# Three-tap branch on GpSimd, transposes without diagonals, and new orders of the start, of the attention mixer and of the expert loop

## The chip, the cores and the metric

The kernel runs on one core of one Trainium2 chip. The metric is the device time of one execution in microseconds. Before the change the median of 3 runs is 2215.55 us (2214.48 to 2218.8).

## The reference

One sequence of 256 tokens with 1024 features, all in float32, passes through two blocks of two layers each.

The first block has two hybrid layers. Each one normalises x, projects it (`w_in`), runs three kinds of heads on it (a gated linear recurrence behind a four-tap convolution, causal attention with 4 heads of 64, and latent attention with 4 heads of 96), joins them with `w_out`, and adds an MLP of 4096 hidden features with a squared ReLU.

The second block is what most of the change touches:

```python
mod = silu(c) @ ada_w[i] + ada_b[i]                  # shifts, scales, gates sh1 sc1 g1 sh2 sc2 g2
h = rmsnorm(x, norm_g[i, 0]) * (1 + sc1) + sh1
y = conv_mixers(h) if i == 0 else attn_mixers(h)
x = x + g1 * y
h = rmsnorm(x, norm_g[i, 1]) * (1 + sc2) + sh2
x = x + g2 * hier_moe(h)

def conv_mixers(h):
    gate_b, gate_c, x_a, val_b, glu_gate = split(h @ w_in)          # 5 x 512 features
    y_a = gate_b * conv3(gate_c * x_a)                              # the three-tap branch
    u = conv31(val_b * sigmoid(glu_gate)) + bias                    # the 31 taps
    y_b = silu(layernorm(u, ln_g, ln_b))
    return concat([y_a, y_b]) @ w_out
```

`attn_mixers` has two kinds of heads over all 256 tokens: eight heads of 64 whose keys are limited to the 64 largest scores of a small index (8 heads of 32), and four differential heads (two softmax maps each, one subtracted with a factor lambda, then an RMS norm over 128). `hier_moe` picks for each token one group of 8 experts and two experts in it; each of 32 experts is a gated MLP of 512 hidden features. A last RMS norm ends it.

## The kernel before, in words

The program is written engine by engine, each with a fixed order of instructions, and the engines meet at semaphores only. A float32 product takes two TensorE instructions, a transpose one. Token tiles are t = 0, 1 of 128 tokens; `xres` holds x, `hT` its normalised transpose (8 tiles k of 128 features by 256 tokens), `bank` the eight PSUM banks, `B(i)` one of them. Intermediate results pass through banks 0 to 3 as numbered jobs (`JOBS`, `JOBS2`): TensorE fills one (`job_filled`), ScalarE drains it (`job_drained`), and a job may start when the one four before it is drained.

Weights pass through `ring`, slots of 2 MB. SyncE issues their loads in a fixed order, each behind a wait that its slot has been used.

Start (L381 to L436): SyncE loads x, then the condition vector, `ada_b`, small columns and positions, waits for GpSimd's constants (`consts`), loads 9 row pieces and 8 small pieces (`layer_small`), and then the first five ring units. TensorE (L757 to L786) turns the condition vector, waits for all the small pieces, turns the rows, turns x (`raw_transposes`) and starts with unit 0, `U_QK`. VectorE forms the rotary tables (L1671 on) before anything else.

Convolution mixer (TensorE L984 to L1001, VectorE L1998 to L2082): five projections `ab0` to `ab9`, two gate-row jobs, then `out_part(0)` for the three-tap half of `mixT`, products with ones for the layer norm (`ln_mu`, `ln_var`), and `out_part(1)` for the other half. VectorE starts the 31 taps when the inputs are drained, runs 24 of them over four channel groups of 256 tokens each (`conv_b(0, 24)`), then the three-tap branch (L2062 to L2067), and then the last 7 taps, centring, square, reciprocal and product, each over all 1024 columns.

`updated` (L1732, VectorE) adds a mixer's or the experts' output to x, one tile t of 1024 columns at a time, and squares it for the norm; GpSimd takes the root (`power2`, L620). `diagonal` puts the root on a diagonal matrix `dg2`, and `norm2` (L929, TensorE) multiplies x by it, which transposes and scales at once; `norm_drains` on ScalarE and `turned_drains` on VectorE scale it by columns into `hT`.

Experts (`moe`, TensorE L1003 to L1138): logits, a chain of small VectorE operations that picks experts and slots, then a loop `quad` over 8 groups of four experts, in two pairs each. Two experts of a pair share a product, one in each half of the array (`product`, L1056). A pair needs six ring slots: gate, up and down for both experts; SyncE refills a slot as soon as `g_filled`, `u_filled` or `y_filled` tells that it has been used (`moe_pairs`, L479). `gather` (L1041) brings tokens to the experts' slots by a product with a 0/1 matrix times the root (`pick`), `scatter` (L1050) adds the results back. VectorE also adds up the relative bias of the later attention in the first loop (`bias_of`).

Attention mixer (TensorE L1151 to L1241): gate row, index queries and keys, 8 index scores (`rel`), the projections `qc` to `vd`, and then four groups g of scores, softmax, transposes and values in turn; then lambda and norm, four transposes `cm`, and two output products. VectorE's softmax stands at L2298 to L2311, ScalarE's exponents at L1538 to L1547.

## Time and profile before

| what | us |
|---|---|
| median of 3 runs | 2215.55 |
| the profiled execution's own time | 2216.15 |
| its span, first to last instruction | 2214.4 |
| TensorE (PE) busy | 2063.9, 93% |
| VectorE (DVE) busy | 911.5, 41% |
| ScalarE (ACT) busy | 354.8, 16% |
| GpSimd (POOL) busy | 88.8, 4% |
| mean granted TensorE clock | 0.969 |

Busy TensorE is not TensorE at full speed: the instructions overlap, and at a granted clock of 0.5 (1.2 instead of 2.4 GHz) the same instruction is busy for twice as long. The profile reads from left to right as first block (to about 788), convolution mixer (to 922), first experts (946 to 1437), attention mixer (to 1686), second experts (1711 to 2202), last norm and store.

### The profile page before, as it was taken

How to read it: one execution, taken by the hardware profiler on the slowest of the kernel's cores; microseconds unless marked ns; L12 is line 12 of the kernel's file. 1: busy time of each engine (PE TensorE's matmuls, PEld its weight loads, DVE VectorE, ACT ScalarE, POOL GpSimd, SP SyncE). 2: the span in 40 equal slices, each digit the busy share in tenths (PEclk: the TensorE clock that was granted, in tenths of full speed). 3: DMA queues.
4: the chain of work that ended last, by engine and by line, in shares of the span. 5: the costliest groups of instructions: out<-in, count | busy, mean ns of one | idle time of the engine just before them, and what ended most of it. 6: DMA issues, size and time to landing. Idle time of an engine off the chain costs nothing. (4 is left out here: it accounts for less than half of the span.)

```text
span 2214.4 us, 21599 instructions
## 1 busy us (share of the span) xinstructions
PE 2063.9 (93%) x8170; PEld 1170.3 (53%) x8170; DVE 911.5 (41%) x1817; ACT 354.8 (16%) x744; POOL 88.8 (4%) x178
## 2 busy tenths in 40 slices
PE   6999999998999998699999999989878999999997
PEld 4556666555666676444444444367565444444442
DVE  3354551335455169466676667631334110111102
ACT  1421000132100000111111111111330111111110
POOL 1111110011111000000000000000000000000000
PEclk9999999999999999899999999979769999999999
DMA  6427884243688543269999999924211899999995
GB/s 227 152 79 266 313 321 165 93 149 112 249 304 304 182 150 152 79 260 410 411 408 408 408 424 415 363 82 145 83 76 76 341 411 409 408 408 410 408 408 237
DMA packets 109524, 592.65 MB, mean 268 GB/s; under 512 B 16664, under 2 KB 21271, under 8 KB 84887
## 3 DMA queue, kind: packets, MB, share of 16 engines
q1 hardware_dynamic: 96406, 541.48, 60.8%
q0 software_dynamic: 13056, 50.33, 6.0%
q8 instruction: 41, 0.67, 0.1%
q14 instruction: 21, 0.16, 0.0%
HBM read 590.74 MB, written 1.05 MB: 267 GB/s over the span
## 5 line engine op out<-in xcount | busy, mean ns | idle before, releaser
L1060 PE MATMUL bank<-ring,work 128*64 128x512 f32 x3072 | 676.4, 594 | 25.2 <-ACT work L1477 14.2
L1060 PEld LDWEIGHTS bank<-ring,work 128*64 128x64 f32 x3072 | 227.8, 137 | 439.1 <-issue 425.0
L2203 DVE SCALAR_TENSOR_TENSOR work<-work 128x512 f32<-128x512 f32 x384 | 258.6, 745 | 5.1 <-DVE work L2200 4.9
L731 PE MATMUL bank<-hT,ring 128*128 128x256 f32 x1024 | 223.4, 379 | 3.2 <-DVE hT L1603 3.2
L744 PE MATMUL bank<-ring,work 128*128 128x512 f32 x512 | 222.3, 592 | 0.0
L731 PEld LDWEIGHTS bank<-hT,ring 128*128 128x128 f32 x1024 | 194.4, 190 | 35.1 <-issue 9.4
L2207 DVE SCALAR_TENSOR_TENSOR work<-work,bank 128x512 f32<-128x512 f32 x32 | 22.0, 688 | 437.4 <-ACT work L1465 437.4
L1952 DVE SCALAR_TENSOR_TENSOR work<-ring,cond,work 128x512 f32<-128x512 f32 x168 | 126.3, 752 | 105.9 <-DMA ring<-in_ada_w 100.7
L744 PEld LDWEIGHTS bank<-ring,work 128*128 128x128 f32 x512 | 97.2, 190 | 115.5 <-issue 114.8
L1046 PEld LDWEIGHTS bank<-work,xres 128*128 128x128 f32 x512 | 124.6, 335 | 27.3 <-issue 22.7
L1046 PE MATMUL bank<-work,xres 128*128 128x256 f32 x512 | 133.5, 414 | 2.9 <-DVEq L2192 2.9
L666 PE MATMUL bank<-ring,hT 128*128 128x512 f32 (+1 forms) x320 | 135.0, 579 | 0.0
L951 PE MATMUL bank<-hT,ring 128*128 128x256 f32 x608 | 135.0, 385 | 0.0
L951 PEld LDWEIGHTS bank<-hT,ring 128*128 128x128 f32 x608 | 117.4, 194 | 17.6 <-issue 1.1
L1052 PE MATMUL bank<-work 128*128 128x512 f32 x256 | 119.6, 600 | 1.4 <-ACT work L1477 1.4
L666 PEld LDWEIGHTS bank<-ring,hT 128*128 128x128 f32 x320 | 59.8, 190 | 68.7 <-issue 68.5
L1458 ACT ACTIVATE work<-bank,modc,work 128x256 f32<-128x256 f32 x128 | 61.9, 564 | 119.9 <-PE bank L1046 119.9
L1052 PEld LDWEIGHTS bank<-work 128*128 128x128 f32 x256 | 46.3, 192 | 54.8 <-issue 51.2
L1382 ACT ACTIVATE work<-bank 128x512 f32<-128x512 f32 x32 | 19.1, 597 | 349.9 <-PE bank L731 349.9
L1477 ACT ACTIVATE work<-bank 128x512 f32<-128x512 f32 x64 | 38.2, 597 | 185.7 <-PE bank L1060 185.7
L2213 DVE SCALAR_TENSOR_TENSOR work<-work,bank 128x512 f32<-128x512 f32 x32 | 22.0, 687 | 110.1 <-PE bank L1060 110.1
L867 PE MATMUL bank<-ring,hT 128*128 128x512 f32 x128 | 59.1, 616 | 4.4 <-ACT hT L1264 2.6
(365 smaller groups left out, 1548.1 us busy)
## 6 DMA issues: line engine op xcount, KB each, us to landing
ring<-in_moe_w_gate SPq DMA_DIRECT2D x64, 2048.0 KB, 11.8
ring<-in_moe_w_up SPq DMA_DIRECT2D x64, 2048.0 KB, 15.3
ring<-in_moe_w_down SPq DMA_DIRECT2D x64, 2048.0 KB, 12.1
ring<-in_ada_w POOLq DMA_DIRECT2D x48, 1024.0 KB, 9.2
ring<-in_w_up SPq DMA_DIRECT2D x16, 2048.0 KB, 13.1
ring<-in_w_down SPq DMA_DIRECT2D x16, 2048.0 KB, 10.0
ring<-in_w_in SPq DMA_DIRECT2D x10, 2048.0 KB, 7.7
ring<-in_cd_w_in SPq DMA_DIRECT2D x6, 2048.0 KB, 8.6
```

The lines of the kernel that those rows point to most:

```text
L666: last = pe.matmul(b[:, 0:n], (hT if x is None else x)[:, k, t * P:t * P + P], w[:, k, 0:n], start=(k == kk - 1), stop=(k == 0))
L731: last = pe.matmul(B(4 + b)[:, (c % 2) * S:(c % 2) * S + S], w[:, k, c * P:c * P + P], hT[:, k, :], start=(k == 0), stop=(k == DT - 1))
L744: last = pe.matmul(B(2 * t + hf), uT[:, u % 2, k, t * P:t * P + P], w[:, k, 512 * hf:512 * hf + 512], start=(u == 0 and k == 0), stop=(u = ...
L867: last = pe.matmul(B(2 * t + hf), mT[:, 4 * u + k, t * P:t * P + P], w[:, k, 512 * hf:512 * hf + 512], start=(u == 0 and k == 0), stop=(u ...
L951: last = pe.matmul(b[:, (c % 2) * S:(c % 2) * S + S], w[:, k, c * P:c * P + P], hT[:, k, :], start=(k == 0), stop=(k == DT - 1))
L1046: last = pe.matmul(b[:, (d % 2) * S:(d % 2) * S + S], xres[:, t, d:d + DT * (P - 1) + 1:DT], pick[:, t, :], start=(t == 0), stop=(t == TT ...
L1052: last = pe.matmul(B(2 * t + hf), pgT[:, t * P:t * P + P], ye[:, 512 * hf:512 * hf + 512], start=False, stop=True, skip_group_check=True)
L1060: last = pe.matmul(b[h, :], x[:, k, h], w[e][:, k, c0:c0 + 512], start=(k == 0), stop=(k == kk - 1))
L1458: ins = act.activation(xeT[:, d, :], b[:, (d % 2) * S:(d % 2) * S + S], ACT.Identity, scale=gm[:, 2 * i + 1, d:d + 1], bias=sh[:, d:d + 1])
L1477: act.activation(ye[:, 512 * hf:512 * hf + 512], (G, U)[hf], ACT.Copy).then_inc(m["y_drained"], 1)
L1952: ins = dve.scalar_tensor_tensor(ada_acc[:, c % 2, :], ada_w[hf][:, k, :], cond[:, kk:kk + 1], ada_acc[:, c % 2, :], ALU.mult, ALU.add)
L2203: mo.do(dve.scalar_tensor_tensor(fl(bias[:, h]), mask_b, rbt[:, bass.ds(12 * bk + h, 1)], fl(bias[:, h]), ALU.mult, ALU.add))
```

## The change

- **Start.** SyncE loads x, the nine row pieces and then the ring units; the other small pieces go out between the ring units (`between`). TensorE turns x and starts unit 0 without waiting for the small pieces; the condition vector is turned between its halves. The tables are formed behind the first norm (`first_tables`), and GpSimd makes the constants that TensorE needs first.
- **First block.** The drains of `hT` are waited for one by one also for k of 4 and 6, and the sums of tile 1 go in halves of 512 columns, with `out_half` and `down_half` counting halves.
- **Norms of the second block.** `norm2` is made of plain transposes (`turn`) of x scaled into `xn` (`scaled_first` on ScalarE, `scaled_second` on VectorE). Ahead of the experts x is turned unscaled; the scale of columns goes into the router's weights (`router`), the root into the logits, and x, scaled and with its features in the order of the gather, is copied to `xn` by ScalarE (`scaled_for_gather`).
- **Convolution mixer.** GpSimd runs the three-tap branch. VectorE runs the 31 taps without a break, and the layer norm goes by channel groups; squares are ScalarE's.
- **Expert loop.** The scatter of a pair stands behind the next pair's hidden product, in both pairs; the gather comes in four pieces before the last down product; a first scatter adds zeros, a last one stands behind the loop.
- **Attention mixer.** Index scores stand between the first projections, the last four projections between the softmax groups, the output's first half before group 3 is done, the gate row behind it. Lambda is applied to the sums' inverses, and the last norm goes by tiles.

The core of the diff:

```diff
+            def short_branch():                                          # GpSimd
+                pool.wait_ge(s2["cols_done"], 1)
+                pool.wait_ge(s2["job_drained"], JOB2["ab7"] + 1)
+                own.do(pool.tensor_tensor(pa[:, :, 2:2 + S], abx[1][:, :, :], abx[2][:, :, :], ALU.mult))
+                own.wait()
+                for w in range(3):
+                    for c in range(4):
+                        tap = colsA[:, A_CA + 4 * w + c:A_CA + 4 * w + c + 1]
+                        own.do(pool.tensor_scalar(abx[2 if w else 1][:, c, :], pa[:, c, w:w + S], tap, None, ALU.mult))
+                    if w:
+                        own.wait()
+                        own.do(pool.tensor_tensor(abx[1][:, :, :], abx[1][:, :, :], abx[2][:, :, :], ALU.add))
+                    own.wait()
+                pool.wait_ge(s2["job_drained"], JOB2["ab9"] + 1)
+                pool.tensor_tensor(mixT[:, 0:4, :], abx[1][:, :, :], abx[0][:, :, :], ALU.mult).then_inc(s2["ya_ready"], 1)
...
-            conv_b(0, 24)                                                # VectorE
-
-            drained("ab7")
-            do(dve.tensor_tensor(pa[:, :, 2:2 + S], abx[1][:, :, :], abx[2][:, :, :], ALU.mult))
-            wait()
-            do(conv(abx[1], pa, 3, 0, 3, lambda w, c: colsA[:, A_CA + 4 * w + c:A_CA + 4 * w + c + 1], None))
-            wait()
-            drained("ab9")
-            dve.tensor_tensor(mixT[:, 0:4, :], abx[1][:, :, :], abx[0][:, :, :], ALU.mult).then_inc(s2["ya_ready"], 1)
-
-            ins = conv_b(24, 31)
-            wait()
-            ins.then_inc(s2["u_ready"], 1)
+            conv_b(0, 30)
+            for c in range(4):
+                dve.scalar_tensor_tensor(abx[3][:, c, :], pb[:, c, 30:30 + S], colsB[:, 120 + c:121 + c], abx[3][:, c, :],
+                                         ALU.mult, ALU.add).then_inc(s2["u_ready"], 1)
+            dve.wait_ge(s2["job_filled"], JOB2["ln_mu"] + 1)
+            total = B(OWN_BANK["ln_mu"])[:, 0:S]
+            for c in range(4):
+                dve.scalar_tensor_tensor(abx[3][:, c, :], total, -1.0 / 512, abx[3][:, c, :], ALU.mult, ALU.add).then_inc(s2["uc_ready"], 1)
...
-            out_part(0, AB_OUT, 6, landed2, mixT)                        # TensorE
+            out_part(0, AB_OUT, 6, landed2, mixT, ROW0 + ROW1[:1])
...
+            over_channels("ln_mu", "u_ready", abx[3])
+            out_part(0, AB_OUT, 6, landed2, mixT, ROW1[1:], 0, 2)
+            over_channels("ln_var", "uq_ready", abx[4])
+            out_part(0, AB_OUT, 6, landed2, mixT, ROW1[1:], 2, 4)
+            pe.wait_ge(s2["y_ready"], 1)
+            out_part(1, AB_OUT, 6, landed2, mixT, ROW0 + ROW1, 0, 1)
+            pe.wait_ge(s2["y_ready"], 4)
+            out_part(1, AB_OUT, 6, landed2, mixT, ROW0 + ROW1, 1, 4)
...
+            def turn(t, src):
+                for c in range(DT):
+                    last = pe.transpose(B(4 + c // 2)[:, (c % 2) * S + t * P:(c % 2) * S + t * P + P], src(c), ident[:, :])
+                    if t == 1 and c % 2:
+                        last.then_inc(s2["xT_filled"], 1)
...
+                    for j in range(2):                                   # quad
+                        pr = 2 * it + j
+                        hidden(it, j)
+                        pe.wait_ge(m["pg_drained"], pr + 1)
+                        scatter(0)
+                        hidden_turned(pr)
+                        scatter(1)
+                        if j == 0:
+                            pe.wait_ge(m["pickg_ready"], it + 1)
+                        gates_turned(it, j)
+                        down(pr, 0)
+                        if more and j == 1:
+                            pe.wait_ge(m["p_ready"], it + 2 + i)
+                            pe.wait_ge(m["pg_drained"], pr + 2)
+                            gather(0, X)
+                            gather(1, T)
+                            pe.wait_ge(m["xt_drained"], 4 * it + 5)
+                            gather(2, X)
+                            pe.wait_ge(m["xt_drained"], 4 * it + 6)
+                            gather(3, T)
+                        down(pr, 1)
...
+            for nm, unit, heads in (("qc0", 1, (0, 1)), ("qc1", 1, (2, 3)), ("kc0", 2, (4, 5)), ("kc1", 2, (6, 7)), ("vc0", 3, ()), ("vc1", 3, ()), ("qd0", 4, ())):
+                projection(nm, unit)
+                for h in heads:
+                    relevance(h)
+            scores2(0)
+            projection("qd1", 4)
+            p_transposes2(0)
+            projection("kd0", 5)
+            values2(0)
+            scores2(1)
+            projection("kd1", 5)
+            p_transposes2(1)
+            projection("vd0", 6)
+            values2(1)
+            scores2(2)
+            projection("vd1", 6)
+            p_transposes2(2)
+            mixed(0)
+            mixed(1)
+            values2(2)
+            scores2(3)
+            drained2("od01")
+            pe.wait_ge(s2["x_done"], 2)
+            out_part(0, CD_OUT, CD_RING, landed3, hT, ROW0)
+            p_transposes2(3)
+            out_part(0, CD_OUT, CD_RING, landed3, hT, ROW1)
+            values2(3)
+            gate_row(["gate1a", "gate1b"], 3)
+            mixed(2)
+            mixed(3)
+            for t in range(TT):
+                drained2("cm%d" % (2 + t))
+                out_part(1, CD_OUT, CD_RING, landed3, hT, (ROW0, ROW1)[t])
```

## Rows read from the trace of the kernel before

**Rows 1.** Page, busy time by engine: us (share of the span) xinstructions.

```profile
PE 2063.9 (93%) x8170; PEld 1170.3 (53%) x8170; DVE 911.5 (41%) x1817; ACT 354.8 (16%) x744; POOL 88.8 (4%) x178
```

**Rows 2.** Windows: stretch, us, each engine's busy us (instructions), PEclk, DMA share, GB/s.

```profile
865.00:921.60 56.60, 37.48 (x81) 17.44 (x80) 28.44 (x51) 7.15 (x10) 0.73 (x2) 0.82 0.44 181
921.60:946.00 24.40, 18.10 (x98) 15.48 (x98) 17.06 (x73) 3.43 (x8) 0.73 (x2) 0.93 0.29 93
946.00:1437.00 491.00, 473.56 (x2016) 211.32 (x2016) 323.68 (x578) 75.31 (x144) 0.00 (x0) 1.00 0.94 393
1437.00:1456.80 19.80, 9.68 (x48) 9.52 (x49) 11.44 (x23) 2.64 (x5) 1.47 (x4) 0.72 0.46 169
1456.80:1686.20 229.40, 207.31 (x770) 150.64 (x768) 61.23 (x124) 51.95 (x130) 2.58 (x4) 0.82 0.22 83
```

**Rows 3.** Start: a transfer (KB, us to landing), then the timeline (start us, us).

```profile
xres<-in_x SPq DMA_DIRECT2D x1, 1024.0 KB, 5.3
...
13.16 16.37 SPq L436 DMA_DIRECT2D ring<-in_w_in  x5
...
22.09 15.92 PE L786 MATMUL bank<-hT,ring 128*128 128x256 f32 x64 [1.76 <-DMA ring<-in_w_in]
```

**Rows 4.** Timeline of the convolution mixer: start us, us, xcount, [idle before <-releaser].

```profile
825.26 39.26 DVE L2045 SCALAR_TENSOR_TENSOR work<-work 128x256 f32<-128x256 f32 x92
...
864.55 1.23 DVE L2062 TENSOR_TENSOR work<-work 128x1024 f32<-128x1024 f32 x1
...
870.40 1.23 DVE L2067 TENSOR_TENSOR xn<-work 128x1024 f32<-128x1024 f32 x1
...
871.73 15.97 PE L972 MATMUL bank<-ring,xn 128*128 128x512 f32 x32 [6.68 <-issue]
...
905.32 1.22 PE L972 MATMUL bank<-ring,xn 128*128 128x512 f32 x1 [9.35 <-DVE xn L2081]
```

**Rows 5.** Timeline: GpSimd (POOL) instructions, alone and beside VectorE's.

```profile
1.33 0.42 POOL L553 MEMSET smask<- 128x384 f32 x1
...
64.27 3.14 POOL L597 TENSOR_TENSOR rstd<-stat,mhalf 128x16 f32<-128x16 f32 x1
64.66 0.68 DVE L1836 TENSOR_TENSOR_SCAN rows<-rows 4x256 f32<-4x256 f32 x1
...
132.54 1.23 DVE L1578 TENSOR_TENSOR work<-xn 128x1024 f32<-128x1024 f32 x1
132.59 1.24 POOL L593 TENSOR_TENSOR stat<-stat,inv_len 128x8 f32<-128x8 f32 x1 [9.93 <-DVE stat L1583]
...
135.79 0.21 POOL L593 TENSOR_TENSOR stat<-stat,inv_len 128x8 f32<-128x8 f32 x1
```

**Rows 6.** One quad of the loop (window; group; transfer) and the projections' timeline.

```profile
1039.50:1100.80 61.30, 59.21 (x252) 26.41 (x253) 40.45 (x73) 9.41 (x18) 0.00 (x0) 1.00 0.97 411
...
L1046 PE MATMUL bank<-work,xres 128*128 128x256 f32 x32 | 8.4, 415 | 0.0
...
ring<-in_moe_w_down SPq DMA_DIRECT2D x6, 2048.0 KB, 12.3
...
793.95 69.31 PE L951 MATMUL bank<-hT,ring 128*128 128x256 f32 x320
```

**Rows 7.** Timeline of TensorE, the normalised transpose ahead of the second experts.

```profile
1689.19 7.92 PE L935 MATMUL bank<-dg,xres 128*128 128x128 f32 x32 [3.03 <-DVE dg L1763]
```

**Rows 8.** Attention mixer: a window, then groups xcount | busy us, mean ns | idle.

```profile
1578.90:1623.30 44.40, 39.23 (x140) 32.02 (x138) 18.13 (x29) 17.28 (x53) 0.00 (x0) 0.50 0.09 38
...
L1190 PE MATMUL bank<-ring 64*128 64x256 f32 x64 | 21.8, 512 | 0.7 <-ACT work L1535 0.7
L1197 PE MATMUL bank<-ident,work 128*128 128x128 f32 x64 | 15.8, 409 | 7.4 <-ACT work L1542 7.4
L1214 PE MATMUL bank<-work 128*128 128x64 f32 x64 | 14.2, 423 | 1.6 <-ACT work L1547 1.6
L1174 PE MATMUL bank<-work 32*128 32x256 f32 x32 | 13.9, 629 | 0.5 <-ACT work L1516 0.5
```

More of the change, by code:

```diff
@@ L699, in o64, with raw_transposes @@
                 return B(7)[:, 256 * t + 64 * h:256 * t + 64 * h + 64]
-            def raw_transposes(use):
+            def raw_transposes(use, between=None):
                 for t in range(TT):
+                    if t == 1 and between is not None:
+                        between()
                     if use == 0:
@@ L1039, in moe, with gather, scatter @@
                 wslot = [ring[:, j, :].rearrange("p (k n) -> p k n", k=4 if j % 3 == 2 else DT) for j in range(6)]
-                def gather(r, banks):
-                    for d in range(4 * r, 4 * r + 4):
-                        b = banks[d % 4 // 2]
+                def gather(piece, b):
+                    for d in (2 * piece, 2 * piece + 1):
                         for t in range(TT):
-                            last = pe.matmul(b[:, (d % 2) * S:(d % 2) * S + S], xres[:, t, d:d + DT * (P - 1) + 1:DT], pick[:, t, :],
-                                             start=(t == 0), stop=(t == TT - 1))
+                            last = pe.matmul(b[:, (d % 2) * S:(d % 2) * S + S], xn[:, t, d * P:d * P + P], pick[:, t, :], start=(t == 0), stop=(t == TT - 1))
                     last.then_inc(m["gathered"], 1)
-                def scatter(t):
+                def scatter(t, ends=False):
                     for hf in range(2):
@@ L1053, in scatter @@
                                          skip_group_check=True)
-                    return last
+                        if ends and (t, hf) != (0, 0):
+                            last.then_inc(m["last_scatter"], 1)
                 def product(b, x, w, k, kk, c0):
@@ L1132, in moe @@
                     pe.wait_ge(m["p_ready"], it0 + 1 + i)
-                    gather(0, (G, U))
-                    gather(1, (X, T))
+                    pe.wait_ge(s2["xn_scaled"], i + 1)
+                    pe.wait_ge(m["y_drained"], 2 * PAIRS * (q + before) + 2)
+                    for piece, b in enumerate((G, U, X, T)):
+                        gather(piece, b)
                     with pe.Fori(0, QUADS - 1) as qd:
@@ L1169, in _, with relevance @@
             filled2(last)
-            drained2("ki")
-            for h in range(8):
+            def relevance(h):
+                if h == 0:
+                    drained2("ki")
                 b = job2("rel%d" % h)
@@ new lines, in _ @@
+            turned_weights(2)
+            for q in range(2):
+                b = j2("cm%d" % q)
+                out2(act.activation(hT[:, 2 * q:2 * q + 2, :], two(b), ACT.Copy))
+            for t in range(TT):
+                b = j2("od0%d" % t)
+                out2(act.activation(xn[:, t, 512:1024], b, ACT.Copy))
+            exponents(3)
+            turned_weights(3)
+            for i in range(2):
+                act.wait_ge(s2["job_filled"], JOB2["gate1" + "ab"[i]] + 1)
+                out2(act.activation(gbc2[:, 512 * i:512 * i + 512], B(OWN_BANK["gate1" + "ab"[i]]), ACT.Copy))
@@ L1560, in _ @@
+            for t in range(TT):
+                name = "cm%d" % (2 + t)
+                act.wait_ge(s2["job_filled"], JOB2[name] + 1)
+                out2(act.activation(hT[:, 4:8, t * P:t * P + P], B(OWN_BANK[name]).rearrange("p (c n) -> p c n", c=4), ACT.Copy, scale=dcol))
             moe(1, n0)
@@ L2297, in _, with softmax @@
             do(dve.tensor_scalar(lam[:, 2:3], lam[:, 2:3], -LAMBDA_INIT, None, ALU.add))
-            for g in range(4):
+            def softmax(g):
                 for i, heads in enumerate(FULL):
@@ L2333, in _, with divided @@
-            dve.wait_ge(s2["rstd_ready"], k + 1)
-            per_group(v, v, rstd[:, k % len(STATS), :], 4, 128).then_inc(s2["lam_ready"], 1)
+            def divided(g):
+                drained("oc%d" % g if g < 2 else "od01")
+                v, width = (heads_of(xn, 256 * g, 4, 64), 64) if g < 2 else (heads_of(xn, 512, 4, 128), 128)
+                do(dve.tensor_tensor(v, v, spread(rsum[:, :, :], 3, width), ALU.mult))
+                wait()
+            softmax(0)
+            inverse_sums(0)
```

751 lines of the change are left out of this document (414 added, 337 removed).

## The prediction

> **What bounds the kernel now.** I read the page's busy times first: TensorE is busy for 93% of the span and no other engine for half of it [rows 1]. So the question is which TensorE time is waste. Then the busy time by stage, which says where [rows 2]: the two expert loops take 491.0 us each at full clock with TensorE busy for 473.6 and the DMA engines at 0.94; the end of the convolution mixer (865 to 921.6) has TensorE busy for 37.5 of 56.6 us at a granted clock of 0.82; the attention mixer (1456.8 to 1686.2) has it busy for 207.3 of 229.4, also at 0.82, which means that much of "busy" is work at 1.2 instead of 2.4 GHz; and the short stretches ahead of the experts (24.4 us, twice) and behind the first experts (19.8 us) are half empty. The chain of waits and the timeline then give what each gap waits for. TensorE sets the end nearly everywhere, so I sum in TensorE time, stage by stage, against the profiled execution: 2216.15 us, of which the span is 2214.4. The median of the runs shown is 2215.55, 0.6 us less; the forecast holds for either.
>
> **Start (-9.3).** The first product waits for ring unit 0, issued at 13.16 behind 24 small transfers and the constants, and begins at 22.09 [rows 3]: 8.9 us from issue to product. The change issues it behind x and nine small rows, some 0.33 us each, so at about 4.2. x itself takes 5.3 us to land (from 0.79, so 6.1); the 16 transposes and the drains behind it need until about 12.3 (they took from 16.65 to 22 before, cold). So both paths meet near 12.8 instead of 22.1. What was hidden before it (tables, condition vector, small columns) moves behind it: VectorE forms the tables while TensorE runs the 15.9 us of unit 0 [rows 3], which covers their some 8 us; the small columns now queue behind three 2 MB loads and land some 21 us in, before VectorE needs them at 28. If that cover were gone, VectorE would be late by as much for the short convolution.
>
> **First block and entry of the second (-4).** Three products after a residual sum wait for two more drains than their first k needs, and for a sum over 1024 columns where halves would do: about 1.1 us each; 0.7 at the entry of the second block.
>
> **End of the convolution mixer (-6).** VectorE's 31 taps cost 0.427 us each (39.26 for 92) [rows 4]; with 120 such, 1.4 for the first four and 1.2 for the gate, it needs 53.9 us from 821.9: 875.8. Today the three-tap branch sits in between, from 864.55 to 871.6: 7.1 us of VectorE, for which TensorE waits 6.68 us [rows 4]. It goes to GpSimd: 4 products or sums over 1024 columns and 12 products over 256. No row shows GpSimd at such a size. Low end: as fast as VectorE, 7.1 us. Nearest row: 384 columns written in 0.42 us [rows 5], 1.1 ns a column; with two inputs I double it, 2.3 us for each of the four, and 0.4 for each of the twelve: 14.0 us. High end: twice that, 28. From 849.4 (its inputs drained) the branch ends, but for the last product, before the last projection is drained at 863.9; ya is ready near 867, no more a bound.
>
> Does it run beside VectorE, though? A GpSimd product over 8 columns takes 0.21 us alone and 1.24 when it meets a 1.23 us VectorE product with both inputs in SBUF, and both end together; against that, VectorE's scan keeps its 0.68 us under a GpSimd power of 3.14 us [rows 5]. So GpSimd waits for VectorE; whether VectorE waits for a GpSimd instruction that reads 256 or 1024 columns no row shows. I take serial use: 875.8 + 14.0 = 889.8 for the last tap; bounds 875.8 (free) and 904 (28 us, serial).
>
> The Trainium skill says more than the trace shows ("SBUF — State Buffer", Who interferes with whom): a VectorE instruction with two SBUF inputs and a GpSimd instruction that reads SBUF exclude each other, and the second blocks fully. This speaks against the change: every tap is such an instruction. The 1.24 us row agrees with it, the scan row does not show it. The skill also gives 4497 ns for a GpSimd sum over 2048 columns ("GPSIMD Engine Reference", Performance versus the Vector engine); by half of that the branch would take 13.8 us.
>
> Behind the last tap everything goes by channel groups: mean (0.5), four centrings (1.7), square, sum and root (2.1), reciprocal (1.75), scale, shift and tanh (3.7): the first piece of y is there after 9.8 us, at 899.6. Today it is 21.8 (883.45 to 905.3), as the mean waits for a whole 16 us product that had itself begun late and at 1.2 GHz [rows 4]. Then 13.9 us of output product and some 2 for a cold start: 915.5 for 921.6.
>
> **Ahead of the experts (-6.9, twice).** The normalised transpose is 16 products in 32 instructions, begun after a wait of 3.03 and lasting 7.92 us [rows 7]. Plain transposes take one instruction each (64 for 64 in L1197 [rows 8]) and the first half needs no wait: the logits end near +7.2 us instead of +14.3. But VectorE now reaches them late, since it squares first and clears 1280 more columns: it starts at +8.6. The chain of small operations behind it loses 0.9 (eight picks of 0.23 become two instructions, two additions come in).
>
> **Expert loop (-12.5, twice).** Now 61.3 us for four experts, DMA 0.97 busy with 411 GB/s [rows 6]. Terms that change: the gather reads weights with a stride, 8.4 us for 32 instructions, 0.262 each; from contiguous data they take the 0.2166 of the projections (69.31 for 320), 6.9 [rows 6]: -1.5. The waits for the gate product (0.51) and for the turned hidden (0.69) are now behind a scatter; the wait for y's drain (0.88) comes twice instead of once: -0.3. 61.3 becomes about 59.4. Per layer: 6.9 + 7 x 59.4 + 52.4 + a last scatter of 3.6 (the added one adds zeros at the front) = 478.4 for 490.9. The floor beneath: 25.17 MB at the 428 to 431 GB/s of its full stretches is 58.7 us, so the DMA has 0.7 us left. Down weights now go out 0.9 us before the pair that needs them 18.2 us in; such a load lands in 12.3 [rows 6]. VectorE has its 40 us of bias work per quad inside 59.
>
> **Behind the first experts (-10).** The first projection starts at 1456.88, behind sums, two diagonals and the gate row. With the row moved to the end of the stage, and the scaled copy in place of diagonals, it starts about 11.5 us after the first scatter at 1435.2: 1446.9.
>
> **Attention mixer (-42).** TensorE's work at full clock: 288 projection instructions 62.4; v and the output product 27.7 each; keys of the index 7.4; index scores 6.9 (13.9 now, at half clock); scores 14.9 (21.8 now); transposes 7.6 (15.8 plus 7.4 idle); values 14.8 (24.5); mixed transposes 1.9; gate row 3.7: 175.0 us [rows 8]. Between 1578.9 and 1623.3 the clock stands at 0.50 while TensorE waits for softmax between short bursts [rows 8]. The change puts a 6.9 us projection between scores and transposes and another behind them; a softmax group needs 10.6 us from the scores' start, and 3.7 + 6.9 cover just that. The 64 largest of each row take VectorE 15 us behind the last index score; three projections (20.7) cover it. What stays: some 4 us for the last normalisation ahead of mixed(3), 3 of small waits, and I allow 5 for short falls of the clock behind the narrow products: 187 for 229.4.
>
> Sum: 9.3 + 4 + 6 + 13.8 + 25 + 10 + 42.4 = 110.5, so 2216.15 - 110.5 = 2105.6; I say 2105.
>
> **Rivals.**
> A, the port is free: the last tap at 875.8 and the convolution mixer ends at 901.5: 14 us more, 2091. For it the scan row, against it the 1.24 us row.
> B, the attention mixer stays cold: scores, values and index products are narrow, and the clock fell in such work even where TensorE did not pause (index scores, 1473 to 1490). Each of four groups then pays its 7.3 us twice and part of a projection: about +22, 2127.
> C, the expert loop keeps 61.3 us: any hiccup of the DMA engines uses up the 0.7 us, and they set the pace: +25, 2130.
> D, GpSimd is the bound: 28 us serial put the last tap at 904: +14, 2119; this is the case in which the branch's move does the opposite of what it says.
> E, slower than before: the down weights. Their lead falls to 19.1 us, in each of 32 pairs. From a landing time of 19.1 us on, every further us costs 32; the whole gain is gone at 22.6 us, and 23 us gives 2230. Against it: 12.3 us landed today with the engines at 0.97.
>
> **Numbers.** Forecast 0.45; A 0.17; B 0.15; C 0.12; D 0.07; E 0.04. The range takes in A to C and a case better by a few us than A or worse than C: 2084 to 2138. A difference of 0.2% (4.4 us) is about what a measurement can tell from none: faster 0.95, same 0.01, slower 0.04, since only E, or several rivals with one not seen, undoes 110 us.
>
> **What would show it.** The first product at about 13 us; VectorE's taps at 0.43 us with none of 1 to 2 us among them (A) or with them, beside GpSimd's instructions (forecast); a first output product of the mixer that begins near 867 and the second near 900; 59.4 us a quad, with the idle stretch of the DMA engines gone; no long stretch at 0.5 between the attention's scores; no wait of TensorE for down weights. A total above 2140 would mean that I took a stage for covered which is not, most likely attention or the loop.

## The result and the profile after

The changed kernel takes 2109.02 us (median of 4 runs, 2107.61 to 2110.98) beside 2216.94 us for the kernel before in the same measurement: ratio 0.9514, interval 0.9498 to 0.9531. The forecast was 2105, range 2084 to 2138. The profiled execution has a span of 2109.2 us.

The stages of the profile after, in their order: stretch, length, busy time of TensorE (instructions), its weight loads, VectorE, ScalarE, GpSimd, granted clock, DMA share, GB/s. They answer to [rows 2], but here the stages are cut where a product of TensorE begins or ends.

```profile
12.29:782.15 769.86, 751.99 (x2677) 472.32 (x2678) 328.14 (x578) 126.17 (x278) 75.36 (x103) 0.99 0.58 210
782.15:905.25 123.10, 110.16 (x418) 81.54 (x419) 96.47 (x198) 14.10 (x26) 22.51 (x18) 0.92 0.33 125
905.25:922.38 17.13, 15.50 (x85) 12.02 (x84) 14.94 (x66) 6.70 (x10) 0.74 (x2) 0.80 0.33 123
922.38:1403.24 480.86, 466.26 (x2025) 199.77 (x2024) 319.96 (x579) 77.00 (x144) 0.00 (x0) 1.00 0.96 402
1403.24:1414.74 11.50, 3.86 (x17) 3.16 (x17) 9.06 (x13) 2.31 (x4) 1.48 (x4) 0.62 0.79 291
1414.74:1596.41 181.67, 177.75 (x787) 128.74 (x787) 66.11 (x162) 51.87 (x127) 3.16 (x6) 0.98 0.31 116
1596.41:1615.09 18.68, 14.11 (x85) 10.52 (x84) 15.27 (x67) 6.69 (x10) 0.75 (x2) 0.91 0.29 113
1615.09:2096.64 481.55, 466.60 (x2025) 199.37 (x2023) 49.00 (x164) 76.94 (x144) 0.00 (x0) 1.00 0.93 393
```

Cut at the same events, the two traces give where the 105.2 us of span went (the table's column before is from the timeline of TensorE, at 22.09, 793.95, 921.58, 946.04, 1436.98, 1456.88, 1686.16, 1710.62, 2201.56 and 2214.4 us):

| stage | before | after | measured | forecast |
|---|---|---|---|---|
| up to the first product | 22.09 | 12.29 | -9.8 | -9.3 |
| first block, entry of the second | 771.86 | 769.86 | -2.0 | -4 |
| convolution mixer | 127.63 | 123.10 | -4.5 | -6 |
| ahead of the experts | 24.46, 24.46 | 17.13, 18.68 | -7.3, -5.8 | -6.9, -6.9 |
| expert loops | 490.94, 490.94 | 480.86, 481.55 | -10.1, -9.4 | -12.5, -12.5 |
| behind the first experts | 19.90 | 11.50 | -8.4 | -10 |
| attention mixer | 229.28 | 181.67 | -47.6 | -42.4 |
| end | 12.84 | 12.56 | -0.3 | 0 |

The start and the end of the convolution mixer after, on TensorE (start us, us, what, count, idle before and its releaser). They answer to [rows 3, 4]:

```profile
12.29 8.86 PE L819 MATMUL bank<-hT,ring 128*128 128x256 f32 x32 [2.35 <-DMA ring<-in_w_in]
...
863.79 11.98 PE L1015 MATMUL bank<-ring,xn 128*128 128x512 f32 x24 [7.58 <-issue]
876.91 1.99 PE L1040 MATMUL bank<-work,ones 128*128 128x256 f32 x8 [1.14 <-DVE work L2234]
...
888.56 16.69 PE L1015 MATMUL bank<-ring,xn 128*128 128x512 f32 x32 [3.98 <-DVE xn L2251]
```

TensorE still stands 7.58 us for the three-tap half (6.68 before); what shrank is the last pause, ahead of the second half of the output, from 9.35 to 3.98 us. VectorE and GpSimd meanwhile, from the timelines of the two:

```profile
813.76 1.23 DVE L2228 SCALAR_TENSOR_TENSOR work<-work 128x1024 f32<-128x1024 f32 x1 [11.45 <-ACT work L1533]
815.02 1.38 DVE L2216 TENSOR_SCALAR work<-work 128x256 f32<-128x256 f32 x4
816.44 59.89 DVE L2218 SCALAR_TENSOR_TENSOR work<-work 128x256 f32<-128x256 f32 x116
876.37 1.67 DVE L2234 SCALAR_TENSOR_TENSOR work<-work 128x256 f32<-128x256 f32 x4
...
841.40 2.44 POOL L654 TENSOR_TENSOR work<-work 128x1024 f32<-128x1024 f32 x1 [61.87 <-ACT work L1533]
843.95 8.06 POOL L659 TENSOR_SCALAR work<-work 128x256 f32<-128x256 f32 x8
852.09 2.34 POOL L662 TENSOR_TENSOR work<-work 128x1024 f32<-128x1024 f32 x1
854.53 4.14 POOL L659 TENSOR_SCALAR work<-work 128x256 f32<-128x256 f32 x4
858.75 2.46 POOL L662 TENSOR_TENSOR work<-work 128x1024 f32<-128x1024 f32 x1
861.29 2.40 POOL L665 TENSOR_TENSOR xn<-work 128x1024 f32<-128x1024 f32 x1
```

116 taps take 59.89 us, where at 0.427 us [rows 4] they would take 49.5: 10.4 us more. Which of GpSimd's instructions cost that, the windows of these taps alone show (stretch, length, VectorE's busy us and count of taps, then clock, DMA share and GB/s). Two taps lie in the 2.5 us of a two-input instruction, and one of them lasts nearly all of it. Beside eight single-input products there are 17 taps, one of them only the end of the held one; from one start to the next it is 0.51 us (16 steps in 8.11 us).

```profile
816.40:841.40 25.00, 24.46 (x59) 1.00 0.00 1
841.40:843.90 2.50, 2.50 (x2) 1.00 0.00 0
843.90:852.05 8.15, 8.01 (x17) 1.00 0.01 2
852.05:854.45 2.40, 2.37 (x2) 1.00 0.00 0
854.50:858.70 4.20, 4.13 (x9) 1.00 0.48 53
```

The steps from one tap's start to the next give the whole 10.4 us: the four taps that meet a two-input instruction cost 2.19, 1.95, 2.06 and 2.05 us over 0.427, and the 24 steps beside the twelve single-input products 2.2 us together.

One quad (four experts) of the loop after, 59.7 us at a DMA share of 0.99, and in it the two waits that are left and the gather (they answer to [rows 6]):

```profile
1097.00:1156.70 59.70, 57.84 (x253) 24.80 (x254) 39.95 (x73) 9.62 (x19) 0.00 (x0) 1.00 0.99 421
...
1108.58 13.95 PE L1110 MATMUL bank<-ring,work 128*64 128x512 f32 x64 [0.98 <-ACT work L1590]
...
1134.75 13.95 PE L1110 MATMUL bank<-ring,work 128*64 128x512 f32 x64 [0.88 <-ACT work L1590]
...
1156.54 7.17 PE L1096 MATMUL bank<-work,xn 128*128 128x256 f32 x32
```

And a softmax group of the attention mixer after, from the timeline of TensorE, with no idle time and every instruction at full clock; it answers to [rows 8]:

```profile
1488.32 3.72 PE L1244 MATMUL bank<-ring 64*128 64x256 f32 x16
1491.96 7.17 PE L995 MATMUL bank<-hT,ring 128*128 128x256 f32 x32
1498.98 1.91 PE L1251 MATMUL bank<-ident,work 128*128 128x128 f32 x16
1500.72 7.07 PE L995 MATMUL bank<-hT,ring 128*128 128x256 f32 x32
1507.63 3.68 PE L1273 MATMUL bank<-work 128*128 128x64 f32 x32
```

### The profile page after: what moved, and what is told of

It is laid out like the page before. It is cut to its first block and busy times, and to the rows that moved or that the text cites. A ratio compares the mean times of both kernels' runs of the same rounds, so it can differ in the third digit from the quotient of the medians.

```text
span 2109.2 us, 21681 instructions
## 1 busy us (share of the span) xinstructions
PE 2010.4 (95%) x8126; PEld 1110.8 (53%) x8126; DVE 910.6 (43%) x1837; ACT 364.9 (17%) x747; POOL 112.2 (5%) x195
## 5 line engine op out<-in xcount | busy, mean ns | idle before, releaser
L1101 PE MATMUL bank<-work 128*128 128x512 f32 x272 | 131.1, 606 | 1.4 <-ACT work L1590 1.4
L1096 PE MATMUL bank<-work,xn 128*128 128x256 f32 x512 | 114.7, 382 | 0.0
L1096 PEld LDWEIGHTS bank<-work,xn 128*128 128x128 f32 x512 | 96.0, 190 | 24.9 <-issue 12.5
L1101 PEld LDWEIGHTS bank<-work 128*128 128x128 f32 x272 | 46.8, 191 | 62.6 <-issue 59.4
## 6 DMA issues: line engine op xcount, KB each, us to landing
ring<-in_moe_w_gate SPq DMA_DIRECT2D x64, 2048.0 KB, 13.1
ring<-in_moe_w_down SPq DMA_DIRECT2D x64, 2048.0 KB, 12.1
```

The source lines that it names most:

```text
L1096: last = pe.matmul(b[:, (d % 2) * S:(d % 2) * S + S], xn[:, t, d * P:d * P + P], pick[:, t, :], start=(t == 0), stop=(t == TT - 1))
L1101: last = pe.matmul(B(2 * t + hf), pgT[:, t * P:t * P + P], ye[:, 512 * hf:512 * hf + 512], start=False, stop=True, skip_group_check=True)
```

## The experiments

Each was run beside the kernel before; its median there was 2216.6 us for the first group, 2220.3 for the second and 2220.2 for the third, so totals are compared as ratios. All edits are of the changed kernel, whose own repeat gave:

> The changed kernel again, beside the other three, so that differences of a few us can be read from the same chip: 2109 us by every theory.

Measured: 2110.2 us, ratio 0.9521 (0.9508 to 0.9534), taps 59.90 us, all stages of the mixer as before. Its repeats differ by up to 5 us, at mean granted clocks of 0.981 to 0.987. The traces show where such differences can come from: the clock stood at 0.50 for 6.8 us from 782.9 on, and the ten projections took 72.3 us, as in three other traces; in the other nine that stretch was 3.4 us long and they took 70.2 to 70.7. Edits worth 3 us are therefore read from stages of the profile.

### The three-tap branch

**On VectorE again.**

```diff
-                if n == 1:
-                    short_branch()                # GpSimd
...
-            conv_b(0, 30)
+            conv_b(0, 24)
+            ...                                   # product, 12 taps, product: as in the kernel before
+            conv_b(24, 30)
```

> The changed kernel with the three-tap branch back on VectorE, between its taps 24 and 25. In the changed kernel GpSimd's branch took 22.3 us, and VectorE's 120 taps 10.4 us more than 120 times the 0.427 us they take alone. Theory P (a GpSimd sum or product with two inputs keeps VectorE out, one with a single input hardly): the taps are back at 0.427 us, the branch adds 7.1, so the last tap ends 3.3 us earlier against the start of the taps, and the whole takes about 2106 us. Rival Q (moving the branch is worth the 7.1 us it takes off VectorE, and the longer taps have another cause that stays): 7.1 us later, about 2116.

Measured: 2110.11 us, ratio 0.9516 (0.9503 to 0.9529): in the total no difference from the changed kernel (0.9521), so neither the 2106 us of theory P nor the 2116 of Q. The profile decides between them: the last tap ends 60.9 us behind the start of the taps (the gate's product, at 809.34), against 64.3: 3.4 us earlier, as by theory P, and Q falls. VectorE's time from start to last tap, and the sums behind it:

```profile
809.34 1.23 DVE L2226 SCALAR_TENSOR_TENSOR work<-work 128x1024 f32<-128x1024 f32 x1 [9.33 <-ACT work L1531]
812.02 39.26 DVE L2216 SCALAR_TENSOR_TENSOR work<-work 128x256 f32<-128x256 f32 x92
...
868.55 1.67 DVE L2242 SCALAR_TENSOR_TENSOR work<-work 128x256 f32<-128x256 f32 x4
873.37 1.42 DVE L2247 SCALAR_TENSOR_TENSOR work<-bank,work 128x256 f32<-128x256 f32 x4 [3.15 <-PE bank L1038]
```

Of the 3.4 us 2.3 are lost at once: the mean waits 3.15 us (0.90 in the changed kernel), since TensorE's sums for it stand behind 13.1 us of output products that began at 858.5. The first piece of y is there 73.7 us after the start, against 74.8, and the gather of the first experts begins after 106.5 us, against 108.6 in both traces of the changed kernel.

**Its last product earlier.** The same, GpSimd's call left out again, but between taps 18 and 21, so that TensorE has it 5 us earlier.

```diff
-            conv_b(0, 30)
+            conv_b(0, 18)
+            ...                                   # product and 12 taps
+            conv_b(18, 21)
+            ...                                   # last product, behind ab9's drain
+            conv_b(21, 30)
```

> The changed kernel with the three-tap branch on VectorE between its taps 18 and 21, its last product between 21 and 22, so that TensorE has it at +44 us after the start of the taps instead of +49. With the branch between taps 24 and 25 the last tap came 3.4 us earlier, but the sums for the mean waited 2.2 us behind the branch's output product. Theory: now that wait is gone, the first piece of y is there 3.4 us earlier than in the changed kernel (71.4 instead of 74.8 us behind the start of the taps), and the whole takes 2 to 5 us less: ratio 0.950. Rival (TensorE's clock falls in the longer pause before the mean and takes it back): 0.952.

Measured: 2109.03 us, ratio 0.9512 (0.9492 to 0.9531). That interval holds both the 0.950 of the theory and the 0.952 of the rival; the profile speaks for the rival. On TensorE:

```profile
853.74 10.54 PE L1013 MATMUL bank<-ring,xn 128*128 128x512 f32 x24 [1.56 <-ACT work L1534]
869.46 3.78 PE L1038 MATMUL bank<-work,ones 128*128 128x256 f32 x8 [5.18 <-DVE work L2243]
```

The products ran early and at full clock, and then TensorE stood for 5.18 us; the sums for the mean took 3.78 instead of 1.99 us, in this window of the granted clock:

```profile
867.50:874.40 6.90, 4.94 (x10) 3.53 (x11) 4.18 (x12) 1.05 (x1) 0.00 (x0) 0.51 1.03 442
```

y comes at 73.3 us, not at the 71.4 of the theory. Most of TensorE's idle time was moved, not removed: 1.56 and 5.18 us for 7.58 and 1.14 in the changed kernel, with the fall of the clock behind the longer one.

**Without the taps, and without the sums.** In the first, GpSimd only multiplies the two tiles at the end; in the second the two sums are left out and all products stay.

```diff
-                own.do(pool.tensor_tensor(pa[:, :, 2:2 + S], ...))     # first kernel: all of this
-                for w in range(3):
-                    ...
```

```diff
-                    if w:                                                 # second kernel: this alone
-                        own.wait()
-                        own.do(pool.tensor_tensor(abx[1][:, :, :], abx[1][:, :, :], abx[2][:, :, :], ALU.add))
```

> Leaves out the three-tap sum: GpSimd only multiplies two tiles at the end. Theory P: one two-input GpSimd instruction of 2.4 us is left, the taps lose 2.1 instead of 10.4 us, the last tap ends 8.3 us earlier, total about 2101. Rival (the taps were longer for another reason, such as the weights that land meanwhile): 2109, and the taps stay at a mean of 0.51 us.

> Leaves out the two sums of the three-tap branch; its two products and the 12 single-input products stay. Theory P: two of four blocking instructions go, some 4.2 us of VectorE's time with them: total about 2105; the taps beside the 12 single-input products stay at 0.48 us. Rival (every GpSimd instruction takes from VectorE in proportion to its time): 4.8 of 22.3 us go, 2.2 us of VectorE's.

Measured: 2100.69 us (ratio 0.9478, 0.9463 to 0.9492) and 2105.11 us (0.9499, 0.9484 to 0.9513). VectorE's 116 taps in the first and in the second:

```profile
812.38 51.48 DVE L2208 SCALAR_TENSOR_TENSOR work<-work 128x256 f32<-128x256 f32 x116
```

```profile
813.49 55.47 DVE L2215 SCALAR_TENSOR_TENSOR work<-work 128x256 f32<-128x256 f32 x116
```

Over 49.5 us that is 2.0 us for one two-input instruction of 2.66 us, and 6.0 for two of them and 12 single-input products. With the 10.4 of the changed kernel: each two-input instruction costs VectorE 2.0 to 2.2 us, the 12 single-input products together about 2, of 12.1 us that they run. Theory P holds in both; by the rival of the second kernel VectorE would have lost 8.2 us there. One number in its text is too low: the taps beside the single-input products follow each other at 0.51 us in this kernel too, not at 0.48. The weights that land meanwhile are out as a cause: the four two-input instructions of the changed kernel cost the same at a DMA share of 0.00 and at 0.99.

### The attention mixer

**The last five projections ahead of the softmax groups.**

```diff
+            projection("qd1", 4)
+            ...                                   # kd0, kd1, vd0, vd1
             scores2(0)
-            projection("qd1", 4)
             p_transposes2(0)
-            projection("kd0", 5)
             values2(0)
             ...                                   # the same for kd1, vd0, vd1, and for ScalarE's drains
```

> The changed kernel with the projections qd1 to vd1 ahead of the softmax groups, so that nothing stands between scores, transposes and values of groups 0 to 2. Theory (the interleaved projections cover the softmax): 3 x 6.9 us of idle TensorE, and the granted clock falls to half in the 28 us of narrow products between these pauses, which costs up to as much again: 21 to 45 us, so 2130 to 2154. Rival (the 47.8 us that this stage lost were extra work, such as longer transposes): at most 5 us more, 2114.

Measured: 2137.25 us, ratio 0.963 (0.961 to 0.965), 24 us more than the changed kernel. The stage takes 208.5 us instead of 181.7. The window of the low clock, and a group in it:

```profile
1527.40:1571.80 44.40, 38.80 (x138) 31.99 (x139) 19.26 (x34) 16.94 (x55) 0.00 (x0) 0.50 0.13 55
```

```profile
1528.08 1.12 PE L1251 MATMUL bank<-ident,work 128*128 128x128 f32 x4 [1.39 <-ACT work L1645]
1530.12 1.12 PE L1251 MATMUL bank<-ident,work 128*128 128x128 f32 x4 [0.93 <-ACT work L1645]
...
1534.10 7.09 PE L1273 MATMUL bank<-work 128*128 128x64 f32 x32 [0.83 <-ACT work L1653]
```

The 44.4 us at 0.50 of [rows 8] are back to the microsecond. Idle time proper is 4.9 us in this first group, 2.2 in the second and 0.3 in the third; the rest is the same work at 7.1 instead of 3.7 us. So the interleaved projections are worth 26.8 of the stage's 47.6 us, and more through the clock than through the pauses that they fill.

**The index scores in one stretch.**

```diff
+            for h in range(8):
+                relevance(h)
             for nm, unit in (("qc0", 1), ...):
                 projection(nm, unit)
-                for h in heads:
-                    relevance(h)
```

> The changed kernel with the eight index scores in one stretch ahead of the projections, as before the change. Theory (a stretch of narrow products with 32 rows lets the granted clock fall, although TensorE doesn't pause): the 8 us of scores take 14 to 16, and the next projection begins at half clock: about 8 us more, 2117. Rival (the clock stays, the order only hid the drains): 1 to 2 us more, 2110.

Measured: 2118.05 us, ratio 0.9549 (0.953 to 0.9568); the stage takes 187.8 us, 6.1 more. The eight scores as one stretch, the projections behind them, and the window of the low clock:

```profile
1428.16 14.02 PE L1219 MATMUL bank<-work 32*128 32x256 f32 x32 [0.53 <-ACT work L1622]
1442.11 29.18 PE L995 MATMUL bank<-hT,ring 128*128 128x256 f32 x128
...
1427.70:1444.80 17.10, 16.64 (x39) 12.65 (x40) 7.61 (x18) 5.18 (x10) 0.00 (x0) 0.50 0.35 123
```

14.02 us against 4 x 1.99: the theory holds in its price, somewhat cheaper than it said. Where the clock fell it has wrong, and so has the prediction's rival B. It fell at 1427.7, in the pause of 0.53 us ahead of the first score; in the kernel before, at 1473.1, 0.1 us behind the first score's start and the same pause. In the profile of the changed kernel it falls at the same place (1429.9), but there a wide projection follows, and it is back after 3.4 us. So it is not shown that the scores let the clock fall; shown is that in one stretch they ran at 0.50 from the first to the last, without a pause, and that the low stretch lasted 17.1 us.

### The expert loop

**Gather with a stride.**

```diff
-                    ins = act.activation(xn[:, t, :].rearrange("p (d n) -> p d n", d=DT), xres[:, t, :].rearrange(...), ...)   # ScalarE
+                    ins = act.activation(xn[:, t, :], xres[:, t, :], ...)
...
-    ... xn[:, t, d * P:d * P + P], pick[:, t, :] ...                                                                       # TensorE
+    ... xn[:, t, d:d + DT * (P - 1) + 1:DT], pick[:, t, :] ...
```

> The changed kernel, but its gather reads the weights with a stride of 8 elements, as before the change. Theory (TensorE sets the loop): 32 instructions go from 0.224 to 0.262 us, 1.2 us for each of 16 quads: 20 us more, 2129. Rival (the DMA engines, 0.99 busy, set the loop): no more than 5 us, 2114.

Measured: 2121.15 us, ratio 0.9562 (0.9543 to 0.9581), 9 us more. A quad is 60.55 us, 0.85 more, and all of it is in the gather's row, 8.02 for 7.17 us. The weight loads behind it take 335 ns each (190 in the changed kernel's page):

```profile
1156.11 8.02 PE L1096 MATMUL bank<-work,xn 128*128 128x256 f32 x32
...
L1096 PEld LDWEIGHTS bank<-work,xn 128*128 128x128 f32 x512 | 123.7, 335 | 12.1 <-issue 11.8
```

Neither number was met: TensorE's time does set the quad, but in one piece the strided gather takes 8.02 us, not the 8.4 of [rows 6], where it was in two pieces. The two loops take 487.5 us each, together 12.6 more than in the changed kernel's profile and 10.9 more than in its repeat's, so the contiguous gather is worth over half of the 19.5 us that the two loops gained.

**Half of the gather.** It leaves out the second token tile.

```diff
-                        for t in range(TT):
-                            last = pe.matmul(..., xn[:, t, d * P:d * P + P], pick[:, t, :], start=(t == 0), stop=(t == TT - 1))
+                        last = pe.matmul(..., xn[:, 0, d * P:d * P + P], pick[:, 0, :], start=True, stop=True)
```

> Leaves out half of the gather (the second token tile): 3.6 us less TensorE work in each quad. Theory (TensorE sets the loop, the DMA floor of 58.7 us is 0.7 below it): the quad falls from 59.4 to about 58.7, where the DMA engines hold it: 12 to 16 us less, 2095. Rival A (only TensorE counts): 57 us less, 2052. Rival B (the DMA engines set it already): 2109.

Measured: 2085.25 us, ratio 0.9404 (0.9384 to 0.9424), 26 us less. The quad is 58.70 us:

```profile
1100.00:1158.70 58.70, 54.88 (x238) 21.46 (x236) 39.91 (x73) 9.42 (x18) 0.00 (x0) 1.00 1.01 429
...
1132.14 7.09 PE L1109 MATMUL bank<-ring,work 128*64 128x512 f32 x32 [1.71 <-DMA ring<-in_moe_w_up]
```

3.6 us less work gave 1.0 us, and a wait for weights has come: the DMA engines hold the quad at 58.7, as the theory said. The total fell by more than the 12 to 16 us foreseen. The two loops account for nearly all of it, with 468.5 and 468.6 us, 12.3 and 13.0 less each: some 7 for seven quads and 3.6 for the half gather ahead of the loop, which the expectation did not count. The rest, some 2 us in each loop, is not traced.

**Each half of y waited for where it is needed.** This is the version to which the profile points: the gate product writes bank G, which held only y's first half, yet waited for both.

```diff
-                    pe.wait_ge(m["y_drained"], 2 * pr + 2)
                     for b, c, name in ((G, 0, "g_filled"), (U, 1, "u_filled")):
+                        pe.wait_ge(m["y_drained"], 2 * pr + 1 + c)
```

> The changed kernel, but a pair's gate product waits only for the drain of the half of y that lay in its bank, and the up product for the other. Theory (the loop's quad is 59.70 us of TensorE's, of which 1.86 are two waits for y's drain, over a floor of 58.7 us of the DMA engines): the waits of 0.88 and 0.98 go, the quad falls to 58.7 and no lower, TensorE then waits for weights; 12 full quads and parts of the others make about 14 us less: ratio to before 0.945. Rival A (TensorE alone sets the loop): 1.86 us for each of 16 quads, 30 us less, 0.938. Rival B (the waits only move to the next product): no change, 0.952.

Measured: 2096.67 us, ratio 0.9459 (0.9439 to 0.9479), 14 us less than the changed kernel by the ratios, as by the theory; the two loops take 473.4 and 473.3 us. The waits of 0.98 and 0.88 us are gone, and one for weights has come:

```profile
1100.00:1158.70 58.70, 57.58 (x256) 24.23 (x254) 39.90 (x73) 9.63 (x18) 0.00 (x0) 1.00 1.01 429
...
1134.84 7.09 PE L1110 MATMUL bank<-ring,work 128*64 128x512 f32 x32 [1.12 <-DMA ring<-in_moe_w_up]
```

**With the early branch on VectorE.**

> Both of these edits in one kernel: by the theories behind them the gains add up, 14 + 3 us less than the changed kernel, ratio to before 0.944, about 2093 us against a before of 2217. Rival: 0.952, no change.

Measured: 2095.81 us, ratio 0.945 (0.9432 to 0.9467). The fastest median of the kernels that compute everything, but not to be told from the half drain alone, as the branch's edit by itself is within the noise; the 3 us that it was to add were not met. Its profile shows how little room this loop has: the loops take 477.3 and 477.8 us there, some 4 more each than with the same edit alone, since the waits for up weights add up to 2 to 3 us more in each, and behind one of them in each loop (2.66 and 2.23 us) the clock stood at 0.50 for 3.4 us. Why the weights came later in this execution no run shows.

### The start

**All small transfers ahead of the first weights.**

```diff
+            for j in range(3):
+                between(j)
             layer_rows(0)
             ...
-                    if l == 0:
-                        between(j)
```

> The changed kernel, with all small transfers issued ahead of the first weights again, as before the change, and TensorE as free to start as it is now. Theory (the issue of unit 0 sets the start): the first product begins at about 22 us instead of 12.3, and all that follows comes 9.5 us later: ratio 0.956. Rival (a later stage absorbs it, as the weights behind it land in time anyway): 0.952.

Measured: 2118.66 us, ratio 0.9555 (0.9534 to 0.9576), 7.5 us more. The first product begins at 20.43 instead of 12.29 us, 8.1 later (9.5 were expected), and by the total no later stage absorbs it:

```profile
20.43 10.09 PE L819 MATMUL bank<-hT,ring 128*128 128x256 f32 x32 [4.55 <-DMA ring<-in_w_in]
```

These weights were issued at 12.56 us, against 4.31 in the changed kernel and 13.16 before the change [rows 3].

## Why the prediction was right

**Start.** Said: first product at 12.8 us. It came at 12.29, still released by the weights, and the order of issues is worth 8.1 us by itself (last experiment). Tables and small columns stayed hidden: VectorE waited 5.15 us for the small columns, until 27.7 us, but TensorE has no pause from its first product to 60 us.

**First block.** Said -4, measured -2.0 in this profile. In eleven of the twelve other traces, whose first block is the same, it took 766.6 to 768.0 us, 3.9 to 5.3 less than before; so the forecast was met there, and the profiled execution lost some of it (in its first block the clock stood at 0.50 for 3.4 us from 13.4 on and for 10.2 us from 511.7 on). No run undid the halves of the sums, so their own worth stays open. One loss recurs: in every trace of the changed kernel and its edits the clock fell between 777 and 788 us, where the ten projections begin, for 3.4 or 6.8 us, and in the one of the kernel before it did not. Just ahead of it TensorE waits 3.13 us for the second scaled tile, where it waited 1.78 and 0.41 us for the two before the change. Here that costs 3 us of the mixer (72.28 against 69.31 us in [rows 6]); the prediction had nothing for it.

**Convolution mixer.** The total came near (-4.5 for -6), and partly by luck: two steps failed in opposite directions. The step "0.4 for each of the twelve" failed: the single-input products took 1.01 us each, so the branch lasts 22.3 us and not 14.0, and TensorE has its half 49.9 us after the start of the taps, not some 45 (867 less 821.9). The step "serial use" failed the other way: VectorE lost 10.4 us, not the branch's whole time, since the four two-input instructions keep it out and the twelve others hardly do. With the true 22.3 us, serial use would have put the last tap at 76.2 us. It came at 64.3 us for 67.9. Over the stage these 3.6 us were offset by 3.0 of the half clock in the projections, 0.7 of a misread start of the taps (the trace before has it at 822.58, not 821.9), 0.7 behind the last tap and 0.8 in the last product, which makes the 1.5 us between -6 and -4.5. Rival A (free, last tap at 53.9) and rival D (28 us, serial) are both out.

The rule of the Trainium skill that I weighed ("SBUF — State Buffer", Who interferes with whom) is borne out for the two-input instructions: the taps that met one lasted 2.45 to 2.58 us. It does not hold for the single-input products, which also read SBUF: beside eight of them the taps went on at one in 0.51 us. There the measurement decides. The 4497 ns of the Trainium skill for a sum over 2048 columns ("GPSIMD Engine Reference", Performance versus the Vector engine), halved as an estimate to 2.25 us, lies 4 to 9% below the 2.34 to 2.46 us of the rows.

What the title's edit is worth follows: 7.1 us off VectorE and 10.4 on it. Against the same kernel with the branch on VectorE it is 3.4 us to the bad at the last tap and 1.1 at y; in the total no difference can be measured. By the two traces the mixer's gain of 4.5 us came from what lies behind the last tap, the work by channel groups: 10.5 us from the last tap to the first piece of y, for 9.8 said and 21.8 before. No run undid that part.

**Experts.** Said 59.4 us a quad, measured 59.70: the term that was mis-sized is the gather, which takes 7.17 and not 6.9 us, as 32 projection products in a row also do here; 69.31 / 320 was too low a price for a group so short. The floor of 58.7 us was right, and two runs stand on it (half of the gather, half drain). Rival C (61.3, any hiccup of the DMA engines) is out: the idle stretch of the DMA engines is gone, their share 0.99. Rival E did not come: no wait for down weights. When the waits of TensorE go, it is the up weights that are late. The two loops missed by 2.4 and 3.1 us. Of each 0.3 is a wrong sum: 6.9 + 7 x 59.4 + 52.4 + 3.6 is 478.7, not 478.4, so the gain said should have been 12.2 in each and the whole 109.9 instead of 110.5. Seven quads at 0.3 more make the other 2.1 us; what the second loop lost beyond them is not known.

**Ahead of and behind the experts.** -7.3 and -5.8 for -6.9 each; the second time TensorE waits 3.95 us for VectorE's picks, the lateness that the forecast named, with less of TensorE's work at low clock to hide it. Behind the first experts -8.4 for -10: the first projection begins some 13.3 us behind the first half of the last scatter, where 11.5 were said. No run undid either of these stages.

**Attention mixer.** Said 187 us, measured 181.7. Mechanism and place were right (the grouped order gives the low stretch back). Of the 8 us allowed for falls of the clock and small waits some 5 were not used: TensorE is busy for 177.75 us, for 175.0 said, and its idle time of 3.9 us is the one said for the last normalisation. Between the falls near its two ends the clock never left 1.00, as this window shows:

```profile
1433.30:1580.10 146.80, 143.41 (x661) 106.51 (x659) 57.98 (x150) 47.62 (x118) 2.42 (x4) 1.00 0.37 138
```

Rival B (narrow products stay cold) is out for this order, though part of its mechanism is real: in one stretch the index scores did run at half clock to their end. Of the 47.6 us the two runs account for 26.8 and 6.1; the other 14.7 (the gate row, the last norm by tiles, the output product's earlier first half) were not separated.

**What is shown of the whole.** Runs that undo a part give back 8.1 us (start), 26.8 and 6.1 (attention) and some 11 to 13 (gather) of the 105.2. The rest is read from the two traces alone. That the total came so near (2109 for 2105) is in part luck: six stages fell short by 1.1 to 3.1 us, 11.7 together, and the attention mixer, 5.2 us better than said, with three small gains of 1.2 together, made up for half of it.

## What to carry to other kernels

When work is moved from VectorE to GpSimd, price it by GpSimd's two-input instructions: beside VectorE instructions that also read two tiles each of them stopped VectorE for nearly its own length (2.0 to 2.2 of 2.34 to 2.66 us), and each single-input product of 256 columns took some 0.2 us from it; so the move pays only if their sum is below what VectorE is spared. Wide products put between narrow ones, or into TensorE's short pauses, counted twice here: they fill the pause and keep the clock for the work around it. And before a loop is called bound by transfers, look which bank a wait protects; here one counter's value was worth 14 us, where the whole reordering of the two loops had given 19.5.

## What the runs showed of the hardware that was not expected

- A GpSimd product of 256 columns with a single input takes 1.01 us beside VectorE's taps and slows these from one in 0.427 us to one in 0.51; one of 1024 columns with two inputs takes 2.34 to 2.66 us, and the tap that meets it lasts 2.45 to 2.58 us. No run shows the single-input product alone.
- A low stretch of 44.4 us came back at its old length when only the order of the attention's products was restored; the clock stood at 0.50 while TensorE was busy for 38.8 of the 44.4 us.
- Eight index scores of 32 rows, back to back, ran at a granted clock of 0.50 for 14.0 us without bringing it back; laid behind wide projections in pairs, each pair took 1.99 us at 1.00.
- A weight load of 128x128 float32 with a stride of 8 elements takes 335 ns, a contiguous one 190, and 32 products of 256 columns with them 8.02 instead of 7.17 us.
